# Compression for two samples at once, with three products for two outputs, and K and V pages loaded apart

## The reference, cut to what matters

```python
for r in range(m):                                  # m = 2 halves of the window
    proj = jnp.einsum('ncsgd,sdh->ncgh', ch + pe[r][:, None, :], w1[r])
    hsum = hsum + proj[:, r:r + n_cmp]              # row c: chunk c with w1[0], chunk c + 1 with w1[1]
return jnp.einsum('ncgh,hd->ncgd', jax.nn.gelu(hsum), w2)
```

## Time and profile before

| | |
|---|---|
| timed runs, median | 1329.25 us |
| profiled execution, its own time | 1329.91 us |
| its span from first to last instruction | 1328.2 us |
| busy of the span | TensorE 97%, VectorE 46%, ScalarE 27%, GpSimd 12% |
| mean granted clock | 0.988 |

### The profile page before, as it was taken

The page is one execution under the profiler, slowest core; times in us unless marked ns, Lnnn a source line. Parts: engine busy times, 40 slices in busy tenths (PEclk is TensorE's granted clock), DMA queues, the critical chain, the costliest instruction groups (busy, mean ns, idle before and its releaser), DMA issues.

```text
span 1328.2 us, 18950 instructions
## 1 busy us (share of the span) xinstructions
PE 1286.2 (97%) x6710; PEld 1001.6 (75%) x6710; DVE 615.8 (46%) x1414; ACT 361.9 (27%) x723; POOL 160.0 (12%) x380
## 2 busy tenths in 40 slices
PE   7999999999999989999999999899999999999999
PEld 6888666777777756766678888578888888888887
DVE  3776532454444424114012210426878788884321
ACT  4766631343443421212100002512221211210000
POOL 1000000111111152244100110022110110100000
PEclk9999999799999998999999999999999999999999
DMA  5431334322232199989465311012222222222240
GB/s 217 162 126 64 119 125 165 101 64 65 87 90 80 50 308 313 313 290 358 162 243 218 111 64 64 17 48 79 80 80 79 82 81 93 80 103 88 87 150 17
DMA packets 79071, 170.11 MB, mean 128 GB/s; under 512 B 10529, under 2 KB 46306, under 8 KB 78082
## 3 DMA queue, kind: packets, MB, share of 16 engines
q1 hardware_dynamic: 60658, 109.89, 24.7%
q10 hardware_dynamic: 13648, 47.49, 9.7%
q0 software_dynamic: 4672, 11.54, 2.6%
HBM read 159.07 MB, written 9.81 MB: 127 GB/s over the span
## 4 chain that ended last, share of the span: by engine, by line
PE 86%; DVE 4%; issue 3%; SPq 3%; ACT 2%; DMA 1%; POOLq 1%; POOL 0%; ACTq 0%; DVEq 0%
PE ps L2361 18%; PE ps L2203 14%; PE ps L2398 11%; PE ps L491 9%; PE ps L1047 8%; PE ps L1524 7%; PE ps L546 3%; SPq L1330 2%; PE ps L984 2%; PE ps L956 2%; PE ps L970 2%; PE ps L473 1%; PE ps L494 1%; PE ps L1624 1%; SPq L1326 1%
## 5 line engine op out<-in xcount | busy, mean ns | idle before, releaser
L2361 PE MATMUL ps<-arena 128*128 128x272 f32 x1120 | 257.1, 392 | 0.5 <-DVE arena L2612 0.5
L2361 PEld LDWEIGHTS ps<-arena 128*128 128x128 f32 x1120 | 212.7, 190 | 44.8 <-DVE arena L2612 1.0
L2203 PE MATMUL ps<-arena 128*128 128x272 f32 (+2 forms) x640 | 149.5, 396 | 0.0
L2203 PEld LDWEIGHTS ps<-arena 128*128 128x128 f32 x640 | 122.6, 192 | 25.8 <-issue 0.5
L491 PE MATMUL ps<-arena 128*128 128x272 f32 x512 | 122.4, 398 | 7.0 <-DVE arena L606 7.0
L1047 PE MATMUL ps<-arena 128*128 128x256 f32 x512 | 124.2, 398 | 3.4 <-DVE arena L1154 3.2
L1524 PE MATMUL ps<-arena 128*128 128x272 f32 x512 | 122.2, 397 | 1.6 <-issue 1.0
L1047 PEld LDWEIGHTS ps<-arena 128*128 128x128 f32 x512 | 98.5, 197 | 31.6 <-issue 14.9
L2398 PE MATMUL ps<-arena 128*128 128x272 f32 x528 | 121.8, 392 | 0.0
L491 PEld LDWEIGHTS ps<-arena 128*128 128x128 f32 x512 | 98.6, 193 | 27.5 <-issue 6.9
L1524 PEld LDWEIGHTS ps<-arena 128*128 128x128 f32 x512 | 96.8, 192 | 29.4 <-issue 10.3
(11 more groups left out here) (347 smaller groups left out, 1552.5 us busy)
## 6 DMA issues: line engine op xcount, KB each, us to landing
arena<-in_w_close SPq DMA_DIRECT2D x68, 512.0 KB, 3.3
arena<-in_pages_cmp SPq DMA_DIRECT2D x128, 128.0 KB, 2.1
arena<-in_past_va ACTq DMA_DIRECT2D x6, 2048.0 KB, 9.4
arena<-in_w_down SPq DMA_DIRECT2D x16, 704.0 KB, 5.8
arena<-in_past_ka ACTq DMA_DIRECT2D x6, 1792.0 KB, 9.9
arena<-in_w_close ACTq DMA_DIRECT2D x16, 512.0 KB, 5.6
arena<-in_w_proj SPq DMA_DIRECT2D x15, 512.0 KB, 3.3
arena<-in_pages_ks SPq DMA_DIRECT2D x80, 64.0 KB, 5.2
```

The source lines that it names most:

```text
L2203: last = pe.matmul(ps[:, 2 * p + a, 0:cols.stop - cols.start], ring[:, chunk % CLOSE_RING, w * P:(w + 1) * P], rhs(k)[:, cols], start=(k = ...
L2361: last = pe.matmul(ps[:, bank(f, i), 0:HALF], w[:, k * P:(k + 1) * P], halved[:, rhs, k, :], start=(k == 0), stop=(k == 3))
```

## The change

A unit of compression is now K or V of two samples (u = 0 to 7; its samples are q = 0 and 1). The chunks are taken as even and odd ones, x[2i] and x[2i+1]. Three products give the two outputs:

- BOTH: x[2i+1] (W0 + W1), for all 64 odd chunks of 2 groups and 2 samples (256 columns)
- EVEN: (x[2i] - x[2i+1]) W0. Added to BOTH it is x[2i] W0 + x[2i+1] W1, row 2i
- ODD: (x[2i+2] - x[2i+1]) W1, 252 columns. Added to BOTH it is row 2i+1

So there are 24 pieces of 8 matmuls in place of 32, spaced nine in sixteen steps. VectorE makes W0 + W1 once, and for each unit the differences: `next_differences` into a buffer of its own, `own_differences` in place, in two halves. Page layout, loads and the order of SP and GpSimd change with it: a page's K and V are loaded apart, 64 KB each (512 B a partition). SP loads both samples of units 0 and 1; from unit 2 on SP loads sample q = 0 and GpSimd q = 1. The constants of the next stage are issued later, since W0 + W1 and the differences lie where they go.

```diff
-    PIECES = NSEQ * 4
+    BOTH, EVEN, ODD = range(3)
+    CMP_UNITS = NSEQ
+    PIECES = 3 * CMP_UNITS
     def pieces_before(t):
-        return min(PIECES, max(0, (t - 4) * 3 // 4))
+        return min(PIECES, max(0, (t - 4) * 9 // 16))
+    def step_of(u, product):
+        return next(t for t in range(STEPS) if pieces_before(t + 1) > 3 * u + product)
+    def seq_step(s):
+        return step_of(2 * (s // 2) + 1, ODD) + s % 2
+    def products(u, product):
+        return 1 + 3 * u + product + 1
...
+    def load_half(queue, engine, u, q, landed):
+        kv, s = u % 2, 2 * (u // 2) + q
+        for p4 in range(NPAGE // 4):
+            at = s * NPAGE + 4 * p4
+            _, found = nc.values_load_multi_w_load_instructions(
+                table[0:1, at:at + 4], engines=(engine,), min_val=0, max_val=d["pages_cmp"].shape[1] - 1)
+            for c, page in enumerate(found):
+                queue.dma_start(pages[:, u % 2, q, 4 * p4 + c, :],
+                                d["pages_cmp"][kv, ds(page, 1)].rearrange("a p n -> p (a n)"))\
+                    .then_inc(landed[u % 2], 16)
 on_sync:
+        def load_pages(u):
+            load_half(sp, mybir.EngineType.SP, u, 0, page_in)
+            if u < 2:
+                load_half(sp, mybir.EngineType.SP, u, 1, page_in)
...
-        sp.wait_ge(m.h_scaled, QT + 1)
-        m.load_constants(sp)
-        for s in range(2, NSEQ):
-            sp.wait_ge(proj_full, 1 + 2 * (s - 2) + 2)
-            load_pages(s)
+        for u in range(2, CMP_UNITS):
+            sp.wait_ge(proj_full, products(u - 2, EVEN))
+            load_pages(u)
 on_pool:
+        for u in range(CMP_UNITS):
+            if u + 2 < CMP_UNITS:
+                pool.wait_ge(proj_full, products(u, EVEN))
+                load_half(pool, mybir.EngineType.Pool, u + 2, 1, page_in_pool)
+            bend(hid_of(u % 2), each_row(inner), 2 + u + 1)
 on_act:
+        def second_half(u):                      # in step_of(u, BOTH)
+            act.wait_ge(proj_full, products(u, BOTH))
+            if u >= 1:
+                act.wait_ge(proj_free, 2 + u)
+            act.activation(second[:, :, :, :], part(BOTH), ACT.Identity, bias=m.cmp_bias[:, u % 2:u % 2 + 1])\
+                .then_inc(second_ready, 1)
+        def bend(u):                             # in step_of(u, ODD) + 1
+            act.wait_ge(inner_ready, 2 + u + 1)
+            act.activation(each_row(bent), each_row(inner), ACT.Tanh, scale=GELU_IN).then_inc(bent_ready, 1)
 on_pe, piece(n):
+            u, product = divmod(n, 3)
+            if product == BOTH:
+                unit_in(pe, u)
+                pe.wait_ge(proj_free, 2 + u)
+                pe.wait_ge(diffs_ready, 1)
+            if product == EVEN:
+                pe.wait_ge(second_ready, 2 + u + 1)
+                pe.wait_ge(diffs_ready, 1 + u + 1)
+            for s1 in range(8):
+                w, rhs, out = {BOTH: (w_both[:, kv, s1, :], x[:, 1, s1], flat),
+                               EVEN: (w1[:, kv, 0, s1, :], x[:, 0, s1], flat),
+                               ODD: (w1[:, kv, 1, s1, :], follows[:, s1, :, :, 0:63], part(ODD)[:, :, :, 0:63])}[product]
+                last = pe.matmul(out, w, rhs, start=(s1 == 0), stop=(s1 == 7))
+            last.then_inc(proj_full, 1)
 on_dve:
+        def add(u):                              # in step_of(u, ODD) + 1, first in the step
+            dve.tensor_tensor(both[:, 0], part(EVEN), second[:, :, :, :], ALU.add)
+            dve.tensor_tensor(both[:, 1, :, :, 0:63], part(ODD)[:, :, :, 0:63], second[:, :, :, 0:63],
+                              ALU.add).then_inc(proj_free, 1)
+        def weights_of_both():                   # in step 2, behind weigh
+            dve.wait_ge(w_in, 16 * 4)
+            dve.wait_ge(m.stored, 16 * 7)
+            dve.wait_ge(m.h_scaled, QT + 1)
+            dve.tensor_tensor(w_both[:, :, :, :], w1[:, :, 0], w1[:, :, 1], ALU.add).then_inc(diffs_ready, 1)
+        def next_differences(u):
+            unit_in(dve, u)
+            if u >= 1:
+                dve.wait_ge(proj_full, products(u - 1, ODD))
+            step.done(dve.tensor_tensor(after[:, :, :, 0:3], x[:, 0, :, :, 1:4], x[:, 1, :, :, 0:3], ALU.subtract))
+            for q in range(2):
+                step.done(dve.tensor_tensor(after[:, :, at, 3], x[:, 0, :, to, 0], x[:, 1, :, at, 3], ALU.subtract))
+        def own_differences(u, q):               # q = 1 gives diffs_ready
+            last = dve.tensor_tensor(x[:, 0], x[:, 0], x[:, 1], ALU.subtract)
...
+                begin = step_of(u - 1, ODD) + 1 if u else step_of(0, EVEN) - 2
+                if t == begin:                   # behind weigh and hidden
+                    next_differences(u)
+                    own_differences(u, 0)
+                if t == begin + 1:
+                    own_differences(u, 1)
 attend_sample, on_sync:
-        sp.wait_ge(m.proj_full, 1 + 2 * (NSEQ - 2) + 2)
+        sp.wait_ge(m.proj_full, m.products(NSEQ - 1, 1))
         for i in range(2):
             for c in range(4):
                 load_pages(sp, SP, 0, c, i, "pages_ks", None if c < 2 else early_in[c - 2])
-        sp.wait_ge(m.proj_full, 1 + 2 * NSEQ)
+            if i == 0:
+                sp.wait_ge(m.proj_full, m.products(NSEQ - 1, 2))
+                m.load_constants(sp)
         for c in range(CLOSE_RING):
             m.load_chunk(sp, c)
 attend_sample, on_pe:
-        pe.wait_ge(m.proj_free, 2 + 2 * NSEQ)
+        pe.wait_ge(m.proj_free, 2 + NSEQ)
         pe.wait_ge(m.s_dve, m.s_dve_uses)
+        pe.wait_ge(m.s_act, m.s_uses - m.s_dve_uses)
```

More of the change, by code:

```diff
@@ L699, in attend_prompt @@
     c_prob_t, c_score = at(39000, 2, T), at(40024, QT, 8, 32)
-    second, inner, bent = at(41048, 2, 2, P), at(41560, 2, 2, P), at(42072, 2, 2, P)
+    second, inner, bent = at(41048, 2, 2, P // 2), at(41560, 2, 2, P), at(42072, 2, 2, P)
     hid = at(42584, 2, 2, 2, P)
+    w_both, x_next = at(43772, 2, 8, P), at(45820, 16, 2, 64)
     table = m.table
     table_in, w_in, mask_in = sem("table_in_p"), sem("prompt_w_in"), sem("prompt_const_in")
-    page_in = [sem(f"cmp_page_in{i}") for i in range(2)]
+    page_in, page_in_pool = ([sem(f"cmp_page_in{e}{i}") for i in range(2)] for e in ("", "_pool"))
     begun, cleared = sem("prompt_begun"), sem("prompt_cleared")
@@ L776, in queries_of, with part, page_view, unit_in @@
         return QA + j if kind == DIL else QB + j
-    def parts(kv):
-        v = ps[:, PROJ, :].rearrange("p (r g c) -> p r g c", r=2, g=2)
-        return v[:, 0], v[:, 1]
+    def part(product):
+        at = 256 if product == ODD else 0
+        return ps[:, PROJ, at:at + 256].rearrange("p (e q i) -> p e q i", e=2, q=2)
+    def page_view(u):
+        return pages[:, u % 2].rearrange("p q n (a w i) -> p w a (q n) i", w=2, i=4)
+    def unit_in(engine, u):
+        engine.wait_ge(page_in[u % 2], 16 * NPAGE * (u // 2 + 2))
+        if u >= 2:
+            engine.wait_ge(page_in_pool[u % 2], 16 * NPAGE * (u // 2))
+    def hid_of(kv):
+        return hid[:, kv].rearrange("p q e c -> p (q e) c")[:, :, 0:NCMP_S]
+    def each_row(v):
+        return v[:, :, :, 0:NCMP_S].rearrange("p q e c -> p (q e) c")
     def p_parts(kv):
@@ L926, in on_act @@
                     small(s)
-                for kv in range(2):
-                    if step_of(4 * s + 2 * kv + 1) + 1 == t:
-                        bend(s, kv)
+            for u in range(CMP_UNITS):
+                if step_of(u, ODD) + 1 == t:
+                    bend(u)
             if 0 <= t - 2 < U:
@@ L936, in on_act @@
                 prompt_second()
-            for s in range(NSEQ):
-                for kv in range(2):
-                    if step_of(4 * s + 2 * kv + 1) == t:
-                        second_half(s, kv)
+            for u in range(CMP_UNITS):
+                if step_of(u, BOTH) == t:
+                    second_half(u)
     def on_pe(pe):
@@ L1163, in cmp_evict @@
+        def own_differences(u, q):
+            x = page_view(u)[:, :, :, q * NPAGE:(q + 1) * NPAGE]
+            if q == 0:
+                step.wait()
+            last = dve.tensor_tensor(x[:, 0], x[:, 0], x[:, 1], ALU.subtract)
+            if q == 0:
+                step.done(last)
+            else:
+                step.wait()
+                last.then_inc(diffs_ready, 1)
         def cmp_evict():
@@ L1212, in on_dve @@
         for t in range(STEPS + 4):
-            for s in range(NSEQ):
-                for kv in range(2):
-                    if step_of(4 * s + 2 * kv + 1) + 1 == t:
-                        add(s, kv)
+            for u in range(CMP_UNITS):
+                if step_of(u, ODD) + 1 == t:
+                    add(u)
             if t == P_PROJ + 1:
@@ L1226, in on_dve @@
                 m.scale_h(dve, QT - 1)
+            if t == P_PROJ + 1:
+                weights_of_both()
             if t == P_PROJ + 3:
                 prompt_hidden()
[L1229 to L1232 removed]
+            for u in range(CMP_UNITS):
```

(4 more changed lines are left out.)

93 lines of the change are left out of this document (33 added, 60 removed).

## The result

The changed kernel takes 1376.31 us (median of 4 runs, 1371.61 to 1382.16), the kernel before beside it 1327.99 (4 runs, 1324.36 to 1329.29): ratio 1.0366, 95% interval 1.0343 to 1.039, slower. The forecast was 1358 in a range of 1334 to 1378. The profiled spans are 1374.4 and 1328.2, so 46.2 us are to be explained where 29 were forecast. (One execution of a run further down, e2, took 2206.67 us at a granted clock of 0.555; it is left out of that run's median, and e2's trace is of it.)

The account below looks back on a forecast made before the run. TensorE was taken as the prompt stage's bound (busy 146.2 of 148 us), with SP's issue list a second path, already later into the sample stage. Terms -29 + 2 + 33 + 19 + 4 = +29 gave 1358, range 1334 to 1378.

Parts of the forecast that it names:

- the two new waits: TensorE's turns wait 3 to 8 us for ScalarE's copy behind GpSimd's bend; the first gate waits about 16 for SP.
- Fewer products: TensorE, prompt stage: 24 pieces in place of 32, -29 us; the new operand pattern costs nothing.
- w_both: VectorE's one addition of 2048 columns in step 2, ahead of an eviction idle TensorE depends on: +2 us.
- Waits in the stage: Prompt stage: TensorE waits for ScalarE's copy, behind GpSimd's late bend and VectorE's differences: +33 us, between 13 and 45.
- 8, 6.1 and 2.8 by shape: TensorE's turn waits: 8 us behind unit 0, 6.1 each at units 2 and 5, 2.8 each at 1, 3, 4.
- Into the sample stage: SP issues sample pages, constants and chunks later, so gates and page scores wait: +19 us.
- SP's list: SP's issues from EVEN(7): first gate chunk issued 35.1 us later, landed at 39 to 42; TensorE there at 23.5.
- what I added for the later pages: Page scores start 55 to 61 us after EVEN(7), TensorE by itself at 39.5; loss 16 to 21 us.
- Clock: TensorE runs slower after some new gaps in the prompt stage: +4 us, between 0 and 12.
- Half of eight, 1.7 us each: Clock term's sizing: half of eight new TensorE gaps each slow the piece behind by 1.7 us.
- the third rival: GpSimd later still: VectorE hinders it, adding 2 us to each of six loads; +12, clock 4 more, 1374; chance 0.13.
- my 10 us: Clock term by the skill's rule, nearly each of eight TensorE gaps costing: about 10 us, sum 6 higher.

Follow-up runs that it names:

- e2: Changed kernel with SP's first sample key pages waiting for EVEN(6) and the constants issued behind all 32 pages: 1362.97 us, ratio 1.0277.
- e4: Changed kernel with 75 unread products of 256 columns put into TensorE's six long waits: 1366.21 us, ratio 1.0275.
- e6: Changed kernel with GpSimd's bend first and SP's sample pages early, plus VectorE's first own difference one step and w_both two steps later: 1323.39 us, ratio 0.9982.
- e1: Changed kernel with GpSimd bending unit u before issuing its 16 page loads of unit u + 2: 1342.38 us, ratio 1.0131.
- e9: e7 with all sixteen of SP's last key pages ahead of the weight chunks and key units: 1324.39 us, ratio 0.9965.
- e11: e9 with TensorE's wait for the constants behind the first gates and the first key unit ahead of the constants: 1323.15 us, ratio 0.9975.
- e7: e6 with ScalarE's Tanh behind its copy of turned weights in the same step: 1325.13 us, ratio 0.9966.
- e10: e9 with 12, 12 and 8 unread products of 128 by 128 in three remaining TensorE waits: 1321.84 us, ratio 0.9949.

## Why the prediction was right, and where it was not

The mechanism was right in each of its places: the two new waits, their engines and their order. The sum was 17 us short. By its terms, from the two traces:

- *Fewer products*, -29. The pieces take 92.9 us with the gaps filled (e4) against 124.2: -31. Both sums hold a few slow pieces. The runs of 4 floats cost nothing that shows: at full clock a piece has the 3.72 us it had the earlier trace rows.
- *w_both*, +2: measured 2.2 (3.71 against 1.50 us at that turn; e6).
- *Waits in the stage*, +33. TensorE's idle time in the stage rose from 10.9 to 51.8 us, 40.9 with w_both's 2.2, so 38.7. The forecast of 8, 6.1 and 2.8 by shape stands against 9.31, then 7.42 and 7.57, then 5.11, 3.71 and 5.34. Each is 0.9 to 2.5 us more, because the bend starts 16 us behind EVEN and not 14.8, and because in two of the six units it takes 4.3 and 4.5 us beside VectorE's differences (3.1 in the others) and not 3.2. EVEN(7) waits 3.15, forecast 3.3. These seven come to 41.6; TensorE's other gaps come to 10.1, and 10.9 of the kernel before and w_both's 2.2 go off. By e1, 25 us of this term are GpSimd's order; 14 stay with GpSimd in time, which are VectorE's, hidden behind GpSimd's here as the forecast had it.
- *Into the sample stage*, +19: 15.4 (46.2 less the stage's 30.8). SP's list was right to the tenth in its sum, with parts off by up to 0.8 us against each other. The 15.8 us of wait are the whole loss; what I added for the later pages was not there: the page scores wait 0.71 us where they waited 1.39 before, and SP issued the last sixteen pages in 14.8 us and not 18.6.
- *Clock*, +4: this is the mis-sized term. The stage's busy time fell by 10.1 us where fewer pieces alone make 31.3, so some 21 us are work at the lower clock. "Half of eight, 1.7 us each" failed twice. The clock was lower behind all of the gaps, not half of them; and it was lower for all of the work of the next steps, as at 355.20 (eight transposes 1.94 us, 1.04 in the earlier trace rows) and for the piece at 482.21 (5.38), and not for one piece. I had taken the one gap in front of a piece as the price of all, and the gap without a fall (470.8 to 473.6) as evidence against. e4 shows the size: with the six long gaps filled, the real work of the stage takes 18.9 us less.

The sum is -31.3 + 2.2 + 38.7 + 15.4 + 21.2 = 46.2; it closes because the third, the fourth and the last of these are what is left of idle time, span and busy time, and e1 and e4 are their checks. The forecast fell short by the 17 us of the clock term alone: the other four terms were off by -2.3, +0.2, +5.7 and -3.6, which cancel. That they cancel is luck, and so is it that 1376.31 lies inside the range, whose upper end of 1378 was made for the third rival. The Trainium skill ("TensorE: Matmul & The Clock Gate", "Why this matters for your kernels") asks for no idle gaps over some 3 us between bursts. By that rule nearly each gap costs; the trace agrees for the gaps of 3.15 to 9.31 us here, and my 10 us for it were still half of what they cost. But gaps under 3 us cost too: the 1.77 of the earlier trace rows, and in e9 one of 1.61 us, behind which eight transposes take 1.94. And a fall comes with no gap at all, in the changed kernel as in the one before (there the piece at 260.23 takes 5.41 us): behind 64 short products of 31 columns the clock is 0.50 from 258 to 262.

```profile
254.84 4.04 PE L1052 MATMUL ps<-arena 64*128 64x31 f32 x64
258.80 6.66 PE L1084 MATMUL ps<-arena 128*128 128x256 f32 x16
```

The third rival named GpSimd's loads as slowed by VectorE, at 1374. Its time came out, its mechanism hardly: four issues take 2.29 to 2.39 us here, near the 2.29 of the earlier trace rows, with VectorE busy or quiet. The pauses between them are 1.34 to 2.14 us, so that the loads are about 1 us longer than forecast and not 2, and the term of the waits is 6 us larger and not 12. The rest of what that rival asked for, the clock took.

VectorE's 41 us more (615.8 to 656.8) were forecast as 40; with GpSimd in time they are a cost of their own, 8 us of it by the place of w_both and of one difference in each unit (e6).

Not settled: whether the bytes that the DMA engines move bound the way into the sample stage, as e9 and e11 suggest, since no run moves fewer; by which waits e11's 5.7 us are lost between 505 and 672; whether e7 is worth anything, since its stage is shorter and its time is not; and an order of the way into the sample stage in which both constants and pages are in time.

## What to carry to other kernels

A load issued by a compute engine is work in its order: sixteen page loads are 14 to 16 us during which nothing behind them on GpSimd happens, and if a short operation behind them feeds a copy that the bound engine needs each step, put that operation first. Price every new gap of TensorE twice, as idle time and as the work behind it at half clock (here 41 us of idle time and 21 of slower work), or test it by filling the gap. Once such waits are gone, look at the next full resource before another reordering: from 465 to 490 the DMA engines were busy 0.99 to 1.06 of the time (e7), and two reorderings there (e9, e11) moved the wait and hardly the end.

## What was not expected of the hardware

More work made the kernel faster: 33.4 us of unread products in the gaps took 10 us off (e4), and 32 products probably 2.6 (e10). And an operation on GpSimd that started together with w_both's addition lasted until just after it. Without that addition, in the kernel before, the same operation takes 0.32 us. VectorE's row, and the rows of GpSimd's operation beside it and of the same one alone:

```profile
234.00 2.28 DVE L1207 TENSOR_TENSOR arena<-arena 128x2048 f32<-128x2048 f32 x1
```
```profile
234.01 2.44 POOL L872 TENSOR_TENSOR arena<-arena 128x62 f32<-128x62 f32 x1
...
237.12 0.32 POOL L872 TENSOR_TENSOR arena<-arena 128x62 f32<-128x62 f32 x1
```
